# Retention and differential-attention block, fp32 on one core: score products read runs of 32 words, turns read contiguous columns

## The reference, cut to what matters

```
proj  = rmsnorm(x) @ w_in                      # 18432 columns: rq rk rv rz dq dk dv dz g_ret g_diff
o_ret  = rmsnorm(retention(rotary(rq), rotary(rk), rv)) * silu(rz)        # 8 heads, dk 128, dv 256
o_diff = rmsnorm(diff_attention(rotary(dq), rotary(dk), dv)) * 0.8 * silu(dz)   # 8 heads x 2 parts of 128
mixed  = sigmoid(g_ret) * (o_ret @ w_ret_up) + sigmoid(g_diff) * (o_diff @ w_diff_up)
out    = rmsnorm(x + mixed @ w_out)
```

## Time and profile before

| what | value |
|---|---|
| median of 3 runs | 1121.41 us (1120.37 to 1121.58) |
| the profiled execution: its time / its span | 1120.17 us / 1118.4 us |
| granted TensorE clock, mean | 0.998 of full speed |
| busy: PE, PEld, DVE, ACT, POOL | 1105.0, 916.1, 677.7, 516.0, 46.9 us |
| moved by DMA | 227.69 MB, mean 204 GB/s |

### The profile page before, as it was taken

The page is one execution under the profiler, slowest core; times in us unless marked ns, Lnnn a source line. Parts: engine busy times, 40 slices in busy tenths (PEclk is TensorE's granted clock), DMA queues, the critical chain, the costliest instruction groups (busy, mean ns, idle before and its releaser), DMA issues.

```text
span 1118.4 us, 12881 instructions
## 1 busy us (share of the span) xinstructions
PE 1105.0 (99%) x4822; PEld 916.1 (82%) x4822; DVE 677.7 (61%) x785; ACT 516.0 (46%) x640; POOL 46.9 (4%) x64
## 2 busy tenths in 40 slices
PE   8999999999999999999999999999999999999997
PEld 7888888888888888888888888888888888888785
DVE  6665456484456545566656756575667676677554
ACT  6544455433445443333544354535553464444443
POOL 0100000000000000000010001000100010000111
PEclk9999999999999999999999999999999999999999
DMA  9876667666666655667566756766677566666853
GB/s 338 261 254 176 193 182 208 190 201 210 171 171 200 210 194 198 189 176 244 148 205 195 210 179 193 217 198 192 187 210 215 180 201 195 202 223 203 324 195 107
DMA packets 141030, 227.69 MB, mean 204 GB/s; under 512 B 14372, under 2 KB 40232, under 8 KB 140200
## 3 DMA queue, kind: packets, MB, share of 16 engines
q1 hardware_dynamic: 140408, 223.72, 65.4%
q10 hardware_dynamic: 560, 3.15, 0.7%
HBM read 210.58 MB, written 2.10 MB: 190 GB/s over the span
## 4 chain that ended last, share of the span: by engine, by line
PE 96%; DVE 1%; DMA 1%; issue 1%; SPq 1%; ACT 0%; ACTq 0%; POOLq 0%; POOL 0%; DVEq 0%
PE bank L990 30%; PE bank L991 30%; PE bank L992 30%; PE bank L1064 1%; PE bank L1068 1%; PE bank L1020 1%; PE bank L999 1%; PE bank L998 1%; PE bank L997 1%; DMA raw<-w_in_dram 1%; SPq L326 0%; PE bank L1021 0%; DVE w_lo L671 0%; DMA rot<-squares_t 0%; ACT w_hi L483 0%
## 5 line engine op out<-in xcount | busy, mean ns | idle before, releaser
L671 DVE TENSOR_TENSOR w_lo<-raw,w_hi 128x1024 fp32r<-128x1024 f32 x383 | 472.8, 1241 | 408.4 <-ACT w_hi L483 407.1
L483 ACT ACTIVATE w_hi<-raw 128x1024 fp32r<-128x1024 f32 x383 | 405.6, 1060 | 560.0 <-PE bank L992 508.3
L990 PE MATMUL bank<-w_hi,xt_hi 128*128 128x512 f32 x1280 | 503.2, 393 | 3.3 <-DVE w_lo L671 2.5
L991 PE MATMUL bank<-w_lo,xt_hi 128*128 128x512 f32 x1280 | 498.9, 390 | 0.0
L992 PE MATMUL bank<-w_hi,xt_lo 128*128 128x512 f32 x1280 | 498.8, 390 | 0.0
L990 PEld LDWEIGHTS bank<-w_hi,xt_hi 128*128 128x128 f32 x1280 | 241.0, 188 | 53.3 <-issue 2.9
L992 PEld LDWEIGHTS bank<-w_hi,xt_lo 128*128 128x128 f32 x1280 | 240.5, 188 | 50.1
L991 PEld LDWEIGHTS bank<-w_lo,xt_hi 128*128 128x128 f32 x1280 | 240.8, 188 | 49.5
L991 PE MATMUL bank<-w_lo,ot_hi 128*128 128x512 f32 x256 | 99.7, 389 | 0.0
L992 PE MATMUL bank<-w_hi,ot_lo 128*128 128x512 f32 x256 | 99.7, 389 | 0.0
L990 PE MATMUL bank<-w_hi,ot_hi 128*128 128x512 f32 x256 | 99.7, 389 | 0.0
(11 more groups left out here) (97 smaller groups left out, 391.9 us busy)
## 6 DMA issues: line engine op xcount, KB each, us to landing
raw<-w_in_dram SPq DMA_DIRECT2D x287, 512.0 KB, 4.1
raw<-w_ret_up_dram SPq DMA_DIRECT2D x32, 512.0 KB, 4.3
raw<-w_diff_up_dram SPq DMA_DIRECT2D x32, 512.0 KB, 4.2
raw<-w_out_dram SPq DMA_DIRECT2D x32, 512.0 KB, 4.1
rot<-squares_t SPq DMA_DIRECT2D x96, 64.0 KB, 2.2
qT<-squares_t SPq DMA_DIRECT2D x48, 64.0 KB, 2.1
kT<-squares_t SPq DMA_DIRECT2D x48, 64.0 KB, 2.1
gate<-x_dram SPq DMA_DIRECT2D x2, 1024.0 KB, 8.2
```

Source lines behind the costliest of these rows:

```text
L483: act.activation(w_hi[:, s, :, :], raw[:, s, :, :], ACT.Copy).then_inc(hi_ready, 1)
L671: dve.tensor_tensor(w_lo[:, s, :, :], raw[:, s, :, :], w_hi[:, s, :, :].bitcast(F32), ALU.subtract) \
L990: pe.matmul(bank[bk][:, :], hi, w_hi[:, s, kk, :], start=k == 0, stop=False)
L991: pe.matmul(bank[bk][:, :], hi, w_lo[:, s, kk, :], start=False, stop=False)
```

## The change

The stationary side keeps its form (`left_tokens` is the old `tokens_of` for one block). The moving side of the score products (`right_tokens`) now reads a tile that is laid out as strip, head, 32 tokens: runs of 32 contiguous words, one run each 128 words. So that the DMAs stay as they are, the tile that is to be read so is written by `turn_squares` without the gap of 4 words (`words_apart` False). In retention the moving side is `qT`, in differential attention `kT`. `mixed_up` is the new read order of the turns: column n*128 + 32j + c, neighbours contiguous. It puts column 32j + c on partition 4c + j. For scores both sides are mixed alike; for the up and out projections the rows of the three weight matrices are permuted on the host in the same way. The attention weights' turn keeps both old orders.

```
-            both = rot[:, :, :].rearrange("p b (t m) -> p m b t", m=QT)
+            both = rot[:, :, :].rearrange("p b (i m r) -> p m (b i) r", i=STRIPS, r=SQUARE)
...
-        def tokens_of(t, m, b0, b1):
-
-            return t[:, b0 * P:b1 * P, m]
+        def head_t(m):
+
+            return rot[:, m % 2, :].rearrange("p (i k r) -> p k i r", i=STRIPS, r=SQUARE)
+
+        def by_strips(t):
+
+            return t.rearrange("p k (s r) -> p k s r", r=SQUARE)
+
+        def left_tokens(t, m, b):
+
+            return t[:, b * P:(b + 1) * P, m]
+
+        def right_tokens(t, m, b0, b1):
+
+            return t[:, :, :].rearrange("p t m -> p (t m)").rearrange("p (s m r) -> p s m r", m=QT, r=SQUARE) \
+                [:, b0 * STRIPS:b1 * STRIPS, m, :]
...
-                               rot[:, m % 2, :].rearrange("p (t k) -> p k t", t=P), ACT.Copy) \
+                               head_t(m), ACT.Copy) \
...
-            def turn_squares(slot, event, src, size):
+            def turn_squares(slot, event, src, size, mixed_up, words_apart):
...
-                dve.transpose(squares_t[:, slot, 0:STRIPS * size].rearrange("p (j c n) -> p j n c", j=STRIPS, c=SQUARE),
-                              src.rearrange("p (n c j) -> p j n c", c=SQUARE, j=STRIPS)).then_inc(squares_ready[slot], 1)
+                to = squares_t[:, slot, 0:STRIPS * size]
+                to = to.rearrange("p (j c n) -> p j n c", j=STRIPS, c=SQUARE) if words_apart \
+                    else to.rearrange("p (j n c) -> p j n c", j=STRIPS, c=SQUARE)
+                src = src.rearrange("p (n j c) -> p j n c", c=SQUARE, j=STRIPS) if mixed_up \
+                    else src.rearrange("p (n c j) -> p j n c", c=SQUARE, j=STRIPS)
+                dve.transpose(to, src).then_inc(squares_ready[slot], 1)
...
-                turn_squares(b, event, rot[:, 0, :], P)
+                turn_squares(b, event, rot[:, 0, :], P, True, words_apart)
...
-                turn_squares(m % 2, event, normed[:, m % 2, :, :, :].rearrange("p e b t -> p (e b t)"), P)
+                turn_squares(m % 2, event, normed[:, m % 2, :, :, :].rearrange("p e b t -> p (e b t)"), P, True, False)
...
-                        rotate(0, it * 4 + (s - 10), 0, ret_uses(it, 0), s - 10, ret_turns(it, 0))
+                        rotate(0, it * 4 + (s - 10), 0, ret_uses(it, 0), s - 10, ret_turns(it, 0), False)
...
-                        rotate(0, it * 4 + (s - 14), 2, ret_uses(it, 0), s - 16, ret_turns(it, 1))
+                        rotate(0, it * 4 + (s - 14), 2, ret_uses(it, 0), s - 16, ret_turns(it, 1), True)
...
-                        turn_squares(a, diff_turns(it, 2), attn_of(a), 3 * SQUARE)
+                        turn_squares(a, diff_turns(it, 2), attn_of(a), 3 * SQUARE, False, True)
...
-                    turn_squares(b, tail_turns(j), mixed[:, b, j * COLS:(j + 1) * COLS], P)
+                    turn_squares(b, tail_turns(j), mixed[:, b, j * COLS:(j + 1) * COLS], P, True, False)
...
-                            pe.matmul(dst[:, 0:2 * P], tokens_of(kT, m, 0, 1), tokens_of(qT, m, 0, 2), start=True, stop=True)
+                            pe.matmul(dst[:, 0:2 * P], left_tokens(kT, m, 0), right_tokens(qT, m, 0, 2), start=True, stop=True)
...
-                            mm = pe.matmul(bank[6][:, c * 2 * P:(c + 1) * 2 * P], tokens_of(qT, 2 * a + c, 1, 2),
-                                           tokens_of(kT, 2 * a + c, 0, 2), start=True, stop=True)
+                            mm = pe.matmul(bank[6][:, c * 2 * P:(c + 1) * 2 * P], left_tokens(qT, 2 * a + c, 1),
+                                           right_tokens(kT, 2 * a + c, 0, 2), start=True, stop=True)
...
+    mixed_up = np.arange(D).reshape(KT, STRIPS, SQUARE).transpose(0, 2, 1).reshape(D)
...
+        if name in ("w_ret_up", "w_diff_up", "w_out"):
+            a = np.ascontiguousarray(a[mixed_up])
```

More of the change, by code:

```diff
@@ L520, in read_ot_hi @@
                 act.wait_ge(turned[m % 2], TURN * (event + 1))
-                act.activation(ot_hi[:, head * 2:head * 2 + 2, :].rearrange("p k (b t) -> p (k b) t", b=BLOCKS),
-                               rot[:, m % 2, :].rearrange("p (t k) -> p k t", t=P), ACT.Copy) \
+                act.activation(ot_hi[:, head * 2:head * 2 + 2, :].rearrange("p k (b i r) -> p (k b) i r", b=BLOCKS, i=STRIPS),
+                               head_t(m), ACT.Copy) \
                    .then_inc(ot_hi_ready, 1)
@@ L624, in read_mt_hi @@
                 k = 4 * j + 2 * half
-                act.activation(xt_hi[:, k:k + 2, :].rearrange("p m (b t) -> p m b t", b=BLOCKS), mixed_t(half), ACT.Copy) \
+                act.activation(by_strips(xt_hi[:, k:k + 2, :]), mixed_t(half), ACT.Copy) \
                    .then_inc(mt_hi_ready, 1)
@@ L835, in _ @@
                         group_done(n0 + 7)
-                        rotate(1, it * 4 + (8 + s - 8), 6, diff_uses_high(it, 0), s - 8, diff_turns(it, 0))
+                        rotate(1, it * 4 + (8 + s - 8), 6, diff_uses_high(it, 0), s - 8, diff_turns(it, 0), True)
                     if s in (16, 17):
                         group_done(n0 + 15)
-                        rotate(2, it * 4 + (8 + s - 14), 2, diff_uses_low(it, 0), s - 16, diff_turns(it, 1))
+                        rotate(2, it * 4 + (8 + s - 14), 2, diff_uses_low(it, 0), s - 16, diff_turns(it, 1), False)
                     if s in (23, 25):
@@ L910, in read_mt_lo @@
                 k = 4 * j + 2 * half
-                dve.tensor_tensor(xt_lo[:, k:k + 2, :].rearrange("p m (b t) -> p m b t", b=BLOCKS), mixed_t(half),
-                                  xt_hi[:, k:k + 2, :].rearrange("p m (b t) -> p m b t", b=BLOCKS).bitcast(F32),
+                dve.tensor_tensor(by_strips(xt_lo[:, k:k + 2, :]), mixed_t(half),
+                                  by_strips(xt_hi[:, k:k + 2, :]).bitcast(F32),
                                   ALU.subtract).then_inc(mt_lo_ready, 1)
@@ L1019, in _ @@
                             dst = bank[6 + m % 2]
-                            pe.matmul(dst[:, 0:2 * P], tokens_of(kT, m, 0, 1), tokens_of(qT, m, 0, 2), start=True, stop=True)
-                            pe.matmul(dst[:, 2 * P:3 * P], tokens_of(kT, m, 1, 2), tokens_of(qT, m, 1, 2), start=True, stop=True) \
+                            pe.matmul(dst[:, 0:2 * P], left_tokens(kT, m, 0), right_tokens(qT, m, 0, 2), start=True, stop=True)
+                            pe.matmul(dst[:, 2 * P:3 * P], left_tokens(kT, m, 1), right_tokens(qT, m, 1, 2), start=True, stop=True) \
                               .then_inc(filled[6 + m % 2], 1)
@@ L1063, in _ @@
                         for c in range(2):
-                            mm = pe.matmul(bank[6][:, c * 2 * P:(c + 1) * 2 * P], tokens_of(qT, 2 * a + c, 1, 2),
-                                           tokens_of(kT, 2 * a + c, 0, 2), start=True, stop=True)
+                            mm = pe.matmul(bank[6][:, c * 2 * P:(c + 1) * 2 * P], left_tokens(qT, 2 * a + c, 1),
+                                           right_tokens(kT, 2 * a + c, 0, 2), start=True, stop=True)
                         mm.then_inc(filled[6], 1)
                         for c in range(2):
-                            mm = pe.matmul(bank[7][:, c * P:(c + 1) * P], tokens_of(qT, 2 * a + c, 0, 1),
-                                           tokens_of(kT, 2 * a + c, 0, 1), start=True, stop=True)
+                            mm = pe.matmul(bank[7][:, c * P:(c + 1) * P], left_tokens(qT, 2 * a + c, 0),
+                                           right_tokens(kT, 2 * a + c, 0, 1), start=True, stop=True)
                         mm.then_inc(filled[7], 1)
```

8 lines of the change are left out of this document (4 added, 4 removed).

## The result

The changed kernel takes **1106.98 us** at the median of 4 runs (1106.66 to 1108.5), beside 1120.89 us for the kernel before; the ratio is 0.9875, with a 95% interval of 0.9864 to 0.9887. The forecast was 1108.2 us, a gain of 13.2; measured are 13.9. The profiled execution is the longest of the four (1108.5 us, its span 1106.7); the part on the clock at the start (e9 and e10) says why.

What follows compares the result with a forecast made beforehand. PE's matmuls were taken to bound the kernel. Score blocks (12.1 us) and the tail's wait (1.1) sum to 13.2 us, taken from 1121.4 us, which carries over 1.2 from the median: 1108.2 us, range 1101.5 to 1112.

Steps and rivals of the forecast that it cites:

- What bounds the kernel: Whole kernel: PE's matmuls are the path, busy 1105.0 of 1118.4 us; DVE and ACT work counts only where PE waits.
- The strided load sets the pace: Score blocks: stationary loads at 0.231 us set the pace; block 1.73 us in place of 2.74, 12.1 us in all; 68%.
- Rival (1): Score blocks: loads hide and the matmuls' own pace counts; 18.5 us gained with the tail, 1102.9 us; chance 17%.
- Rival (2): Score blocks: loads and fast moving reads disturb each other, or whole load records count; 6.5 us gained, 1114.9 us; chance 8%.
- Rival (3): Score matmuls: slow for a reason other than the stride, so only the tail gains; 1120.3 us; chance 4%.
- Rival (4): Score matmuls: each new run of 32 words costs PE time, making the kernel slower; 1128.8 us at 0.045 us; chance 3%.
- The turns: DVE transposes: 0.4 us gained in each of 36, 0.2 in 12 still writing with gaps; hidden beside PE, costed at nothing.
- The tail: First `w_out` group, before unit 6: PE's wait for `xt_lo` goes, gaining 1.1 us (0.9 to 1.1), with nothing late next.
- The signs: Changed profile: score instructions about 0.23 us each, load records still 0.31 us, no new PE wait, clock as now.
- test of a tenth: Score blocks: prediction wrong if the 256-column and 128-column instructions differ in pace by more than a tenth.
- other test: Tail: prediction wrong if another wait of PE has come up in the place of the removed one.
- The sum: Whole kernel: 12.1 us from score blocks plus 1.1 from the tail, 13.2 us gained, giving 1108.2 us.

Runs made afterwards that it cites:

- e9: e1 with 18 transposes of the identity on PE in its first pause, after the first unit; 1102.15 us median.
- e10: e1 unchanged, run again on the same chip as e9; 1103.50 us median.
- e3: Turn side of the change alone; both sides of the scores read words 4 apart as in the kernel before; 1120.37 us, ratio 0.9991.
- e1: The changed kernel with the stationary side of the scores also laid out by heads, so its loads read contiguous words; 1102.47 us median.
- e6: e1 with the stationary side reading every 2nd word in retention, every 3rd in differential attention (wrong words); 1104.93 us, one execution.
- e5: e1 with the moving side reading every 2nd word in retention, every 3rd in differential attention (wrong words); 1108.03 us, one execution.
- e4: e1 with the moving side of the scores read as one contiguous run, of wrong tokens and heads; 1103.82 us, one execution.
- e8: The changed kernel unchanged, run once more for a second profile; 1107.1 us.
- e2: Score side of the change alone; turns, hi and lo read 4 apart as in the kernel before, weights unpermuted; 1109.45 us, ratio 0.9897.

## Why the prediction was right, point by point

- **What bounds the kernel**: right. e3 shows it from the other side: some 20 us less on DVE and 12 on ACT by the groups, and 1120.37 us.
- **The strided load sets the pace, at 0.231 us**: right. 0.92/4 = 0.230; the block was to take 1.73 us and takes 1.75, the gain was to be 1.01 us a block and is 1.01 by the distance of two blocks: 12.1 us. e1 shows the cause by taking it away, e6 by taking away a part of it.
- **Rival (1), the loads hide**: out; its block of 1.29 us comes only with contiguous loads (e1: 1.31). The rule of the Trainium skill that a matmul may begin before its load completes (TensorE: Matmul & The Clock Gate, in its section on the array) did not bring the pace down to the matmuls' own 0.215 and 0.108 us: the loads of L1085, recorded with 0.329 us, follow each other at 0.235.
- **Rival (2), loads and fast reads in each other's way**: out as a bound (0.27 to 0.31 us), though a trace of it may be in the record's 329 in place of 311 ns.
- **Rival (3), the stride costs nothing**: out, by the result and by e5. **Rival (4), a price for each run**: out, by e4.
- **The turns**: 0.41 to 0.42 us gained in each of the 36, as taken (0.4). In the 12 that still write with gaps I took 0.2 and it is at most 0.04: one strided side is enough. Hidden, so without effect on the sum.
- **The tail, 1.1 us, "late next is nothing that the rows show"**: the wait did go, all 1.08 us of it. The second half failed: DVE's wait for the norm's weights is late next and costs PE 0.28 us in the first profile, 0.51 in the second. Net, the tail gave 0.8 and 0.57 us, under the 0.9 to 1.1 forecast.
- **The signs.** The prediction's sum gives the last step of a block 0.11 us, so 128 columns should have read 0.81 and not the 0.92 it named; they read 0.83. Its test of a tenth between the two kinds sits just at this (0.230 and 0.208 us), and in retention the starts differ by far more (0.255 and 0.18) while the loads keep their pace: it should have asked for the distance of the loads. By its other test, no new wait in the place of the tail's, it was wrong by 0.28 us. The loads' records were to stay at 0.31 us and are 0.32 to 0.33. The clock was to stand as now and stood at 0.79 from 12 to 20 us; e8, the same kernel, had 1.00, so this is the start's and not the change's.
- **The sum.** 12.1 + 0.8 = 12.9 us from the traces, beside 13.2 forecast. The medians differ by 13.9, the profiled spans by 1118.4 - 1106.7 = 11.7. The start accounts for the rest: the changed kernel's first score block begins at 79.15 us and that of before at 77.93, so 12.9 - 1.22 = 11.7. Against e8, whose clock stayed up and whose first block begins at 77.58, it is 12.1 + 0.57 + 0.35 = 13.0, and the spans differ by 13.1. That the medians give 1.0 us more than these 12.9, and so land near the 13.2, comes as far as the profiles show from how the starts fell in four runs of each, and the 1.2 us that I carried over from the median is of that kind too: luck, and not the mechanism.

## What to carry to other kernels

A plain fp32 matmul here has two prices, and the greater counts: its moving read, and the load of the next stationary operand, which sets a pace of 0.11 us contiguous and 0.23 us at a stride of 4 words. Making only the moving side contiguous brought 1.01 us a block of a possible 1.42 (8.22 - 6.80); before changing a layout, work out both. Once a wait on a chain is removed, read what arrives on the same engine right behind it: here the loads for the end of the kernel.

## What the runs showed of the hardware that I had not expected

- Reads of PE need not be neighbours to go at nearly full pace: contiguous takes 0.215 us, step 2 0.225, step 3 0.34 (e5), step 4 0.457, for 256 columns. The times fit lines of 4 words, but do not prove them.
- DVE's transpose of 512 columns has two paces, 0.71 us with both sides contiguous and 1.08 or more as soon as either one steps by 4 words (e2, e3).
- After PE's pause in the first microseconds the granted clock falls back to 1.2 GHz for a few microseconds in some executions (the changed kernel, e10) and not in others (e8, e1). Between the changed kernel's two profiles this and the start of the second unit move the first score block by 79.15 - 77.58 = 1.57 us. e1's four runs are 1101.35, 1101.73, 1103.21 and 1103.48 us. The kernel before shows the same spread (1119.91 to 1121.99 us, mean granted clock from 0.998 to 0.996). Eighteen transposes whose result nothing reads, put into that pause, hold it up (e9, one profile); the executions lie 0.2 to 1.3 us above e1's shortest, so a small price of theirs is not excluded.
